# A two-layer hybrid decoder trunk on one core: where the bias tile lives, the order of ScalarE's work in an attention block, a third landing buffer for the down projection, and the tile order of one projection

## The reference

```python
proj = h @ w_in                     # gq, gk, gv, gr, ga (gated linear attention), dq, dk, dv
log_a = log_sigmoid(ga @ w_gla_gate + b_gla_gate) / 16
o_g = rms_norm(gla_chunked(gq, gk, gv, log_a)) * silu(gr)      # 4 heads, chunks of 64
# differential attention, 4 heads, blocks of 128 queries:
s = q[:, q0:end] . k[:, :end] * scale + bias                   # two maps m = 0, 1
p = softmax(where(rel >= 0, s, -inf)); a = p[0] - lam * p[1]
o_d = rms_norm(a @ v)
x = x + g1 * rms_norm(concat(o_g, o_d) @ w_out)
gate, up = split(h @ w_gate_up)                                # width 2816
x = x + g2 * rms_norm((silu(gate) * up) @ w_down)
```

## Time and profile before

| what | us |
|---|---|
| median of 3 runs | 2839.43 (2838.8 to 2844.62) |
| the profiled execution, own time | 2840.74 |
| its span, first to last instruction | 2838.9 |
| TensorE matmuls busy | 2627.0 (93%) |
| VectorE busy | 1156.0 (41%) |
| ScalarE busy | 826.9 (29%) |
| mean granted TensorE clock | 0.964 of full |

### The profile page before, as it was taken

How to read it: one execution, slowest core, us unless ns; L and a number is a source line. 1 busy time by engine, 2 the same in 40 slices (tenths; PEclk the granted TensorE clock), 3 DMA queues, 4 the chain that set the end, 5 groups by cost and what they waited for, 6 DMA issues and landing times. The chain is left out here.

```text
span 2838.9 us, 30677 instructions
## 1 busy us (share of the span) xinstructions
PE 2627.0 (93%) x12450; PEld 2122.9 (75%) x12450; DVE 1156.0 (41%) x1839; ACT 826.9 (29%) x1463; POOL 139.7 (5%) x165
## 2 busy tenths in 40 slices
PE   8799879879999999999999996896999999999997
PEld 7578757658788888878767884674878888887875
DVE  0556345555433321135662454556531111113544
ACT  0422234444211111134552123444431111113433
POOL 0001100002000000001010010000200000000000
PEclk9999989989999999999999998997999999999998
DMA  5252110012444411144341112000321111114443
GB/s 196 83 189 86 31 37 23 16 52 97 153 137 133 141 50 48 46 147 165 132 165 52 38 38 45 23 16 25 110 73 52 45 52 45 52 45 141 171 146 136
DMA packets 183992, 243.61 MB, mean 86 GB/s; under 512 B 9531, under 2 KB 141484, under 8 KB 182828
## 3 DMA queue, kind: packets, MB, share of 16 engines
q1 hardware_dynamic: 172556, 200.74, 22.3%
q0 software_dynamic: 11296, 40.92, 4.2%
HBM read 224.05 MB, written 17.58 MB: 85 GB/s over the span
## 5 line engine op out<-in xcount | busy, mean ns | idle before, releaser
L1710 PE MATMUL ps<-hT,wsp 128*128 128x512 f32 (+1 forms) x2080 | 830.3, 399 | 49.3 <-DVE F L1337 39.6
L1712 PE MATMUL ps<-hT,wsp 128*128 128x512 f32 (+1 forms) x2080 | 815.9, 392 | 0.0
L1711 PE MATMUL ps<-hT,wsp 128*128 128x512 f32 (+1 forms) x2080 | 815.3, 392 | 0.0
L1077 DVE TENSOR_TENSOR wsp<-raw,wsp 128x1024 fp32r<-128x1024 f32 (+2 forms) x140 | 168.0, 1200 | 867.4 <-ACT wsp L638 698.6
L1710 PEld LDWEIGHTS ps<-hT,wsp 128*128 128x128 f32 (+1 forms) x2080 | 390.2, 188 | 156.9 <-issue 65.0
L1712 PEld LDWEIGHTS ps<-hT,wsp 128*128 128x128 f32 (+1 forms) x2080 | 389.9, 187 | 88.2 <-issue 1.9
L1711 PEld LDWEIGHTS ps<-hT,wsp 128*128 128x128 f32 (+1 forms) x2080 | 390.4, 188 | 81.3 <-issue 2.0
L638 ACT ACTIVATE wsp<-raw 128x1024 fp32r<-128x1024 f32 x84 | 89.1, 1060 | 778.5 <-PE ps L1712 615.7
L2035 PE MATMUL ps<-hT,asp 128*128 128x512 f32 x1032 | 251.4, 401 | 16.5 <-DVE asp L1608 16.3
L2035 PE MATMUL ps<-wsp,asp 128*128 128x512 f32 x1080 | 255.3, 393 | 4.0 <-DVE asp L1608 3.7
L2035 PEld LDWEIGHTS ps<-hT,asp 128*128 128x128 f32 x1032 | 197.9, 193 | 64.7 <-DVE hT L1600 12.0
(11 more groups left out here) (189 smaller groups left out, 2513.4 us busy)
## 6 DMA issues: line engine op xcount, KB each, us to landing
raw<-in_w_down SPq DMA_DIRECT2D x132, 512.0 KB, 3.5
raw<-in_w_gate_up SPq DMA_DIRECT2D x88, 512.0 KB, 3.8
F<-in_w_mod SPq DMA_DIRECT2D x80, 512.0 KB, 4.7
raw<-in_w_in SPq DMA_DIRECT2D x48, 512.0 KB, 3.8
out_x<-W POOLq DMA_DIRECT2D x32, 512.0 KB, 3.4
W<-out_x POOLq DMA_DIRECT2D x24, 512.0 KB, 5.5
raw<-in_w_out SPq DMA_DIRECT2D x16, 512.0 KB, 3.4
F<-in_w_mod SPq DMA_DIRECT2D x6, 1024.0 KB, 18.8
```

Source lines behind the costliest of these rows:

```text
L1077: v.tensor_tensor(wsp[0:np_, r, 1, 0:w], raw[0:np_, r, 0:w], wsp[0:np_, r, 0, 0:w].bitcast(F32), ALU.subtract).then_inc(s_lo, 1)
L1710: mm(o, a(0), b(0), start=start, stop=False)
L1711: mm(o, a(0), b(1), start=False, stop=False)
L1712: return mm(o, a(1), b(0), start=False, stop=stop)
```

## The change

There are five edits.

1. The bias gets a tile `bias` of its own in the memory of `gaT`, past the first 1024 values. POOL issues its load once the slot `N_WG` has been multiplied, ahead of the eight square-root pieces of the linear attention, and no longer after them.
2. In `head`, `exps(h, b + 1, 1)` moves up to stand right behind `exps(h, b + 1, 0)`, ahead of `outs` and `probs(b, 0)`.
3. From step 22 on, the down weights land in three buffers in turn; the third is a piece of the activations of tile 2, which is no longer needed then. A load waits for step s - 3 in place of s - 2. Its rows are cut into pieces of 128 values. The loads get semaphores of their own.
4. `hi_act(0)`, `hi_act(1)` and `hi_down(0)` move ahead of the last SiLU.
5. In the first slot of `rows(N_GV, ...)` the tiles go 2 to 7, then 0 and 1, and each waits only for the copy that frees its own bank.

```diff
+        bias = sb("bias", [P, HEADS * NEAR], over="gaT", skip=S)
...
+        def raw_of(s):
+            return s % 2 if s < JT else (s - JT) % 3
...
+        def raw_down(s, a, b):
+            r = raw_of(s)
+            if r == 2:
+                return acts[:, 8:16, 2 * P:3 * P].rearrange("p (a b) n -> p a b n", a=a)
+            return raw[:, r, :].rearrange("p (a b n) -> p a b n", a=a, b=b)
...
                 for s in range(DSTEPS):
-                    n = N_DOWN + s
-                    load(l * SLOTS + n, n % 2, raw[:, n % 2, :], wdn[:, l, s % JT, :])
+                    sp.wait_ge(s_lo, l * SLOTS + N_DOWN + s + (1 if s < JT + 2 else 0))
+                    apart(sp)
+                    sp.dma_start(raw_down(s, 4, 2) if raw_of(s) == 2 else raw[:, raw_of(s), :],
+                                 wdn[:, l, s % JT, :].rearrange("p (a b n) -> p a b n", a=4, b=2)
+                                 if raw_of(s) == 2 else wdn[:, l, s % JT, :]
+                                 ).then_inc(s_rd[raw_of(s)], 16)
...
+                pool.wait_ge(s_pe, l * SLOTS + N_WG + 1 + CREDIT)
+                src = bass.AP(tensor=skew.tensor, offset=skew.offset + P - 1,
+                              ap=[[3 * P - 1, P], [P * 3 * P, HEADS], [1, NEAR]])
+                pool.dma_start(bias.rearrange("p (h k) -> p h k", h=HEADS), src).then_inc(s_bias, 16)
                 for t in range(0, NT):
                     pool.wait_ge(s_gms, l * NT + t + 1)
                     rsqrt(S_GRS, S_GMS, HEADS, s_grs)
...
-                pool.wait_ge(s_gC, l * NT + NT)
-                src = bass.AP(tensor=skew.tensor, offset=skew.offset + P - 1,
-                              ap=[[3 * P - 1, P], [P * 3 * P, HEADS], [1, NEAR]])
-                pool.dma_start(F[:, Fbias:Fbias + HEADS * NEAR].rearrange("p (h k) -> p h k", h=HEADS),
-                               src).then_inc(s_bias, 16)
...
                             exps(h + 1, 0, 0)
+                        if b < NT - 1:
+                            exps(h, b + 1, 1)
+                        elif h < HEADS - 1:
+                            exps(h + 1, 0, 1)
                         if b:
                             outs(h, b - 1)
                         elif h:
                             outs(h - 1, NT - 1)
                         probs(b, 0)
-                        if b < NT - 1:
-                            exps(h, b + 1, 1)
-                        elif h < HEADS - 1:
-                            exps(h + 1, 0, 1)
                         if b >= 4:
                             probs(b, 1)
...
+                        if i * 2 + jj == JT - 1:
+                            hi_act(0)
+                            hi_act(1)
+                            hi_down(0)
                         act.wait_ge(s_f2, l * JT + i * 2 + (jj + 1))
                         nc.scalar.activation(W[:, 1024 + 1024 * jj:2048 + 1024 * jj],
                                              pair(2 * jj), ACT.Silu).then_inc(s_f1, 1)
...
-                        for t in range(NT):
+                        for t in (2, 3, 4, 5, 6, 7, 0, 1) if i == 0 else range(NT):
...
                 def free_gv(t):
-                    pe.wait_ge(s_tev, l * 4 + 4)
-                    pe.wait_ge(s_zb, l * 4 + 4)
+                    if t < 2:
+                        pe.wait_ge(s_tev, l * 4 + 4)
+                    elif t < 4:
+                        pe.wait_ge(s_tev, l * 4 + 3)
+                    else:
+                        pe.wait_ge(s_zb, l * 4 + 4)
```

More of the change, by code:

```diff
@@ L53 @@
 SLOT = KT * P
-assert SLOTS % 2 == 0
+assert SLOTS % 2 == 0 and N_DOWN % 2 == 0
+def raw_of(s):
+    return s % 2 if s < JT else (s - JT) % 3
+RAW_USES = [sum(raw_of(s) == r for s in range(DSTEPS)) for r in range(3)]
 P_A, P_B, P_G = 0, 8, 16
@@ L177, in build @@
         Fk, Fv = (4096, 6144), (5120, 7168)
-        Fp, Fat, Fbias = 16384, 20480, 21504
+        Fp, Fat = 16384, 20480
         Fx, Fxn, Fv4, Fj = 0, 8192, 16384, 20480
@@ L215, in wdown @@
             if s % 4 < 2:
-                return wsp[:, s % 4, z, :].rearrange("p (a n) -> p a n", n=2 * P)
+                return wsp[:, s % 4, z, :].rearrange("p (a b n) -> p a b n", a=4, b=2)
             k = 4 * (s % 4 - 2)
-            return hT[:, z, k:k + 4, 6 * P:8 * P]
+            return hT[:, z, k:k + 4, 6 * P:8 * P].rearrange("p a (b n) -> p a b n", b=2)
         def aslot(g, k, z):
@@ L264, in build @@
         s_raw = [sem("s_raw0"), sem("s_raw1")]
+        s_rd = [sem("s_rd0"), sem("s_rd1"), sem("s_rd2")]
         s_hi, s_lo = sem("s_hi"), sem("s_lo")
@@ L317, in raw_in, with down_in @@
         def raw_in(l, n):
-            return l * (8 * SLOTS) + 16 * (n // 2 + 1)
+            return l * (8 * N_DOWN) + 16 * (n // 2 + 1)
+        def down_in(l, s):
+            r = raw_of(s)
+            return 16 * (l * RAW_USES[r] + sum(raw_of(q) == r for q in range(s + 1)))
+        def raw_down(s, a, b):
+            r = raw_of(s)
+            if r == 2:
+                return acts[:, 8:16, 2 * P:3 * P].rearrange("p (a b) n -> p a b n", a=a)
+            return raw[:, r, :].rearrange("p (a b n) -> p a b n", a=a, b=b)
         def kn(a):
@@ L977, in _ @@
                     act.wait_ge(s_st[q], uses_after(l, 0, q))
[L979 to L988, removed]
                 def hi_down(s):
-                    n = N_DOWN + s
-                    act.wait_ge(s_raw[n % 2], raw_in(l, n))
+                    act.wait_ge(s_rd[raw_of(s)], down_in(l, s))
                     before = s - 2 if s < 2 else -1 if s < 4 else s - 4
                     act.wait_ge(s_pe, down_step(l, before) + 1 + CREDIT)
[L997 to L1001, removed]
+                    nc.scalar.activation(wdown(s, 0), raw_down(s, 4, 2), ACT.Copy).then_inc(s_hi, 1)
                 def hi_act(s):
@@ L1012, in hi_act @@
                                          ACT.Copy).then_inc(s_ah, 1)
+                for i in range(0, JT // 2):
+                    for jj in range(2):
+                        if i * 2 + jj < JT - 1:
+                            act.wait_ge(s_pe, l * SLOTS + i * 4 + (N_FF + 2 * jj + 1 + CREDIT))
+                        if i * 4 + 2 * jj + 2 < 2 * JT:
+                            hi_ff(l, i, 2 * jj)
+                        if i * 2 + jj == JT - 1:
+                            hi_act(0)
+                            hi_act(1)
+                            hi_down(0)
+                        act.wait_ge(s_f2, l * JT + i * 2 + (jj + 1))
+                        nc.scalar.activation(W[:, 1024 + 1024 * jj:2048 + 1024 * jj],
+                                             pair(2 * jj), ACT.Silu).then_inc(s_f1, 1)
+                        if i * 4 + 2 * jj + 2 < 2 * JT:
+                            hi_ff(l, i, 2 * jj + 1)
                 def feed(s):
@@ L1025, in y1 @@
                     return yj(l, 1, t)
-                hi_act(0)
-                hi_act(1)
-                for s in range(4):
+                for s in range(1, 4):
                     hi_down(s)
@@ L1364, in maxes @@
                     near = pair(1 + m)[:, n - w:n]
-                    o = Fbias + h * NEAR + NEAR - w
-                    v.tensor_tensor(near, near, F[:, o:o + w], ALU.add).then_inc(s_ba, 1)
+                    o = h * NEAR + NEAR - w
+                    v.tensor_tensor(near, near, bias[:, o:o + w], ALU.add).then_inc(s_ba, 1)
                     dve.wait_ge(s_ba, at + 1)
@@ L2130, in _ @@
                         last = y_mms(1, t, lambda z, k: aslot(g, k, z)[:, i * P:i * P + P],
[L2131 removed]
+                                     lambda zz, k, h: hT[:, zz, 4 * (s % 4 - 2) + 2 * h:
+                                                         4 * (s % 4 - 2) + 2 * h + 2, 6 * P:8 * P]
                                      if s % 4 >= 2 else wsp[:, s % 4, zz, 512 * h:512 * h + 512],
```

6 lines of the change are left out of this document (2 added, 4 removed).

## The result

| | before | changed |
|---|---|---|
| median, us | 2841.89 (4 runs, 2838.80 to 2844.62) | 2800.72 (4 runs, 2796.00 to 2801.21) |
| span of the profiled execution | 2838.9 | 2799.4 |
| mean granted TensorE clock in it | 0.964 | 0.969 |

The ratio is 0.9851, with a 95% interval of 0.9839 to 0.9863: the medians lie 41 us apart, and the ratio says 42. The span fell by 39.5 us.

The account below looks back on a forecast made before the run. TensorE's matmuls, busy 93% of the span, bound the kernel, so only its waits and half clock could be won. -29.1 - 7.2 + 2.1 - 7.0 = -41.2 us on 2840.74 gives 2799.5, said as 2799; 8 in 10: 2788 to 2810.

Parts of the forecast that it names:

- The bias: Before the attention's first values, both layers: loading the bias early removes VectorE's idle wait for it, -29.1 us.
- The values' order: First value slot of each layer: tiles 2 to 7 first remove 2.19 us gaps and half clock behind, -7.2 us.
- clock term: The half clock right behind the first value slot's gap goes with the gap, -2.8 us for two layers.
- The exponentials: Attention, both exponentials first: -1.8 us per layer in heads one to three, +2.9 in the fourth, net +2.1 us.
- Rival (a): In the attention the exponentials' order costs +5 us per layer in place of +1, time 2807; chance 0.12.
- The prediction's sign of being wrong: Wrong if TensorE's first-values wait stays over 8 us at the attention, or the fourth head grows over 5 us.
- The third buffer: Last group of the down projections: third landing buffer removes 5.6 us of waits and 1.4 of half clock, -7.0 us.
- the rule that I had weighed: Last down group: all transfers share 16 engines, so earlier issue gains only if they are free; else 0, not -7.0.
- rival (b): Transfers are the bound in the down projection's last group, so the third buffer gains nothing, time 2806; chance 0.10.
- The SiLU: Start of the down projections: moving first splits ahead of the last SiLU leaves the waits there unmoved, 0 us.
- Rival (e): Slower than before: turned(b, 1) waits in blocks 4 to 7 of every head, over 1.3 us each; chance 0.03.
- Rival (d): More gain: exponentials' waits fall 4 us per layer, clock stays up behind bias, -10 and -4, time 2785; chance 0.06.

Follow-up runs that it names:

- bias_alone: The kernel before with only the bias tile of its own, loaded early: 2810.34 us, ratio 0.9873.
- exps_alone: The kernel before with only the new order of the exponentials (both first): 2846.89 us, ratio 1.0006.
- all_but_gv: The changed kernel with the old order of the value tiles: 2804.90 us, ratio 0.9864 to the kernel before.
- all_but_exps: The changed kernel with the old order of the exponentials: 2796.58 us, ratio 0.9825 to the kernel before.
- where covered: The changed kernel with both exponentials first only in blocks 0 to 3 and 7 of heads one to three and block 0 of the fourth: 2789.63 us, ratio 0.9801.
- all_but_act: The changed kernel with the last SiLU first again, as before: 2798.91 us, ratio 0.9843 to the kernel before.

## Why the prediction was right

The forecast was 2799 and the median is 2800.72. (The sum in the prediction gives 2798.2 when the 1.3 us are taken off, and the kernel before stood at 2841.89 in these runs and not at 2839.43; the difference of 41.2 us is the thing to hold against it.) The spans differ by 39.5 us. The starts of the same matmuls in the two traces account for all of it:

| where, us | first layer | second layer | predicted, both |
|---|---|---|---|
| values' tile order | -3.6 | -2.8 | -7.2 |
| clock, later in the linear attention | +3.3 | 0 | 0 |
| bias wait | -14.9 | -14.6 | -29.1 |
| exponentials, attention to output projection | +1.9 | +2.2 | +2.1 |
| first matmuls of the down projection | -1.4 | -1.3, then +1.3 | 0 |
| third group and end | -3.9 | -5.8 | -7.0 |

This table is of two traces. The means over the traces with and without each edit say more, and come out at -31.2 for the bias, -5.5 for the values' order, +3.5 for the exponentials and -8.9 for the third buffer: -42.1 in all, beside -42 and -46 us by the two timings. The prediction had -29.1, -7.2, +2.1 and -7.0. Each term was off by 1.4 to 2.1 us, two one way and two the other. The mechanisms were right but for the half clock behind the gap; that the total lies within 1 us of the forecast is luck.

**The bias** was right in its place: VectorE's idle time, not TensorE's, was the thing to count, since the short operations between it and TensorE stayed. The two waits shrank by 14.9 and 14.6 us (29.5, for 29.1 forecast) in the two traces, and by 31.2 us against the mean of the four old traces. The transfer itself is quicker in its new place: it lands in 5.5 and 7.4 us, where it took 13.4 and 13.7.

**The values' order** was right in the gaps, 2.19 us in each layer. Its clock term was not. In the two traces it seems to hold at the spot, where the stretch at half clock is gone, and to be paid back further on: the changed kernel has 13.7 us at half clock from 284.9 us on, where the kernel before had 6.8 from 290.7 on, which costs 3.3 us. But that longer stretch can't be put down to the edit: `bias_alone`, with the old order, has the same 13.7 us there, and `exps_alone` and `all_but_gv`, also with the old order, have 10.2. From the first layer's first small projection to the end of its linear attention, the nine traces with the new order are 2.1 us shorter in the mean than the five with the old one, which is the gap; on the mean no clock time is won there. In the second layer the difference is 3.4 us, of which 1.2 could be clock. So the step that was mis-sized is "-2.8 us for two layers" for the half clock behind the gap: some 1 us of it is seen. The timed trials (7 us alone, 7.8 when left out) have intervals too wide to tell 5.5 from 7.2.

**The exponentials** were right in sign in both parts, and the count per block held where I could read it (1.6 us in block 6). In the two traces the first three heads are 1.3 and 1.2 us shorter in the two layers (-1.8 forecast for each), and the fourth, from its first scores on, is 3.1 longer in each (+2.9 forecast). With the output projection that makes the +4.1 of the table, and not +2.1. Over all traces the attention is 1.7 us longer in a layer, +3.5 for both. So the term was too small by 1.4 to 2 us. By the waits the same edit moves far more: 13.7 us went, and 13.7 and 4.4 came. What the hand count had left out is the wait behind the combination: about 2 us of it per layer are one new wait in the fourth head, for `combine(2)`. On VectorE that stands behind `oT_lo`, which waits for ScalarE's `oT_hi`, and this copy is now behind both exponentials. The combination ends 3.9 us after the start of block 3's scores, where it was 3.2 in the kernel before and in `all_but_exps`, so 0.7 us of the wait are the edit's. The rest is no loss: `all_but_exps` waits 1.0 us at this place, and the kernel before, which was at half clock ahead of it, came too late to wait. The "where covered" version shows that covered and uncovered blocks were told apart rightly. Rival (a), at +5 us per layer, is out: it was +2. The prediction's sign of being wrong, a fourth head longer by more than 5 us, did not come: 3.1 us against the kernel before, 4.7 against `all_but_exps`.

**The third buffer** was right in its mechanism and too small: -9.7 by the trace (in which the end of the kernel is included), 8.8 by leaving it out, 8.9 in the mean of the traces, where I had 7.0. The idle time that went is 2.8 us in the first layer and 3.4 in the second, all of the 6.2 and not 5.6: I had kept 0.6 us back for a late last load, of which TensorE saw 0.1. One stretch at half clock went, in the second layer, as counted (1.6 us by the starts, for 1.4). The rest, some 2 us, the prediction did not have: steps of 12 matmuls that took 2.80 to 3.04 us, next to the waits and further on, where they take 2.75 now, at full clock and with hardly any idle time in the record.

Here the rule that I had weighed (the Trainium skill, DMA: Bandwidth & Descriptors, section Issuing engines are not separate DMA queues) would have had the gain at nothing if the engines were the bound. They were as busy as before, 0.92, and the gain came. It was the moment of the issue that was late and not the rate at which the engines worked, so rival (b) is out. That the transfers share is seen here too: a load issued at 1405.62 us in the third group, beside POOL's rows, took 6.4 us to land where 4.3 is the median, and those beside the row fetches at the down starts took 6.2 to 7.0 where it is 3.5.

**The SiLU** edit was put at 0. Its gain cannot be told from 0 (1.8 us, intervals overlapping). Both starts of the down projection stayed, as forecast. The half clock behind them is 6.8 us long in each layer of the kernel before and 3.4 in the changed one, and the -1.4 and -1.3 us of the table are mostly this. The edit is not the cause: `all_but_act`, without it, has 3.4 and 3.4, and `all_but_gv`, with it, has 6.8 and 6.8. No edit goes with these lengths over the 14 traces, so what sets them is open, and that row of the table belongs to no edit.

**Rival (e)**, that `turned` waits at 32 places, is out: the first three heads gained, so `fill` covers them. **Rival (d)** wanted the exponentials' waits down by 4 us per layer; they fell by 6.9, but as much and more came back in the waits behind them.

## What to carry to other kernels

Count a late tile by the idle time of the engine that waits for it first, and check that the operations from there to the bottleneck stay. When an in-order queue is reordered, make the count block by block: the new order is worth having only where TensorE has other work between the two results, and a condition on the block gave both gains here (7 us against the old order everywhere, by the runs timed beside each other; the span is 6 to 11 us shorter than with the edit in every block). Where loads have no slack against the steps, a third buffer can pay although the transfer engines are nine tenths busy, as it did here. And when a term is a few us, hold it against several traces: two of them gave an edit 3.3 us of half clock that other kernels have without it.

## What the runs showed of the hardware

The time of the same code follows the granted clock from run to run. The changed kernel was profiled twice. Within the spans, its two traces have 176.3 and 167.6 us at half clock, in 2799.4 and 2794.4 us (203.2 us before the change). Half of the difference, 4.4 us, is most of the 5 us between the spans. Here are the 18 us around the start of the first attention in the two executions; the second window is moved by the 1.4 us that this execution is ahead:

```profile
346.85:365.00 18.15, 13.43 (x53) 9.64 (x53) 9.86 (x26) 8.13 (x17) 5.42 (x6) 0.81 0.44 97
```

```profile
345.44:363.59 18.15, 13.43 (x58) 9.82 (x58) 9.96 (x26) 8.74 (x20) 5.42 (x6) 0.91 0.42 94
```

The granted clock was 0.81 and 0.91 there, and five matmuls more were started in the second. So a term of 1 or 2 us for one stretch at half clock is below what one trace can tell: 5 us lie between two profiles of the same code.

There is a second, smaller thing. Early in the second down projection the first execution of the changed kernel started 300 matmuls in 69.70 us at a granted clock of 1.00, the second one 306 in the same time:

```profile
2554.30:2624.00 69.70, 69.70 (x300) 56.49 (x299) 29.07 (x33) 24.92 (x34) 0.00 (x0) 1.00 0.41 136
```

```profile
2551.30:2621.00 69.70, 69.70 (x306) 57.22 (x305) 30.23 (x34) 26.05 (x36) 0.00 (x0) 1.00 0.42 136
```

By the starts of the same matmuls, 1.3 us are lost in this stretch, which is what the row of the table above takes back. The times come in two values: 230 matmuls of this stretch take 53.67 us in six of the 14 traces and 52.64 or 52.65 in the other eight, at full granted clock in all, and no edit goes with it. What slows them is not known.
